# A two-block kernel: the first projection with the weights stationary, u made once, the fold done behind the projection

## The chip, the cores and the metric

One core of a Trainium2 chip runs the whole program in one launch. The metric is the device time of an execution in microseconds (us), the median of several runs. The engines are TensorE (PE; its weight loads are PEld), VectorE (DVE), ScalarE (ACT), GpSimd (POOL) and SyncE (SP), which issues most DMAs.

## What is computed

Two transformer-like blocks in a row. The change lies in the first projection, the Fourier branch and the k and v projection of the first block; cut to these, with b = 1:

```python
h = concatenate([meta_tokens, x])                  # 16 + 1024 positions, 1024 wide
u = rmsnorm(h, norm_g)
proj = u @ w_in                                    # f_in (512), f_gate, q, k (128), v (128), a_gate
fr = real(fftn(f_in, axes=(position, channel of a group of 64), norm="ortho"))
f_out = einsum("blgc,gcd->blgd", fr, w_fmix) + b_fmix, times silu(f_gate)
a_out = attention(rope(rmsnorm(q)), rope(rmsnorm(k)), v) * silu(a_gate)
h = h + concatenate([f_out, a_out]) @ w_out        # then a norm and the second block
```

The second block (stick-breaking attention, a gated convolution, a feed-forward part with w_up and w_down) takes most of the time and is not touched.

## The kernel before

Every product of full precision is made of three matmuls in fp32r: each operand is split into a high part, rounded to fp32r, and a low part, the rest, and `three` adds high x high, high x low and low x high (L667, L668, L669). Weights go through a staging pair and a ring of four slots: SyncE loads a chunk of 512 KB, GpSimd's `split` (L559 to L562) writes its high and low parts, and TensorE frees the slot with the semaphore w_used. SyncE loads chunk n once chunk n - 2 is split; GpSimd splits chunk c once chunk c - 4 has been used. Chunks 0 to 3 belong to the first projection, 4 to 7 hold the Fourier tables, 8 and 9 the k and v weights, then come the gates. The order on each engine is written out by hand, and waits are on counting semaphores.

The first 184 us go as follows. (1) x comes in as eight tiles of 128 tokens and one of 16 meta tokens. ScalarE squares and sums them (L1241) and guesses the reciprocal root (L1201, L1203), VectorE refines it in four small instructions (L1829 to L1832) and scales the tile (L1850), TensorE turns it (`transpose_tile`, L677), ScalarE copies it into `u_t` (L1233). (2) The real Fourier transform over 1040 positions needs only the sums and differences of position n and 1040 - n. VectorE forms them from `u_t` for each of the eight groups of 128 features (L1887, L1888), ScalarE and VectorE split them into `u_folded` (L1255, L1879). (3) `tm_units` projects: the folded u is the stationary operand, 512 columns of weights move. The 521 sums and 519 differences are ten row tiles; the fifth and the tenth hold only 9 and 7 rows. (4) Sixteen Fourier products of 15 matmuls, in two halves with eight channel products behind each; the fifth group of three is for the short rests, with `dft_tail`. VectorE makes low parts of the results (`dft`, L1927), then `f_out` (L1937, L1940). (5) x is loaded again, scaled again (L1850), and each tile is turned ahead of the kv unit before its own; the high and low parts of `u` are kept this time (L1311, L1855). (6) After the nine kv units the first two k tiles are turned (`turn_k`, L826), and the other seven amid the gate units, one after every fifteen matmuls; the third needs its rotation (`k_rotated`, L1971).

## Time and profile before

| | |
|---|---|
| median of 3 runs | 2212.61 us (2210.72 to 2220.72) |
| the profiled execution's own time | 2215.88 us |
| its span, first to last instruction | 2214.1 us |
| instructions | 27859 |
| mean granted TensorE clock | 0.985 |

A row of the timeline gives the start in us from the span's start, the busy time, the engine, the line, the instruction with the tiles it writes and reads, and in brackets the idle time of the engine just before with what ended it. Durations of overlapping matmuls are longer than the pitch from one start to the next; the pitch is what counts for a sum. The granted clock is 1.00 at 2.4 GHz and 0.50 at 1.2 GHz.

### The profile page before, as it was taken

The numbers are of one execution on the slowest core, as the hardware profiler recorded it, in microseconds if no ns is written. First come the engines' busy times: TensorE is split into PE (matmuls) and PEld (weight loads), VectorE is DVE, ScalarE is ACT, GpSimd is POOL, SyncE is SP. The second block draws the span as 40 slices with busy tenths as digits, with TensorE's granted clock in tenths as the row PEclk, the third lists the DMA queues.
The fourth block names the chain that finished last, engine by engine and source line by source line (L and its number), as shares of the span: only waits on it lengthen the run. The fifth ranks groups of instructions, "written<-read, shape, count | busy, mean of one in ns | idle before, by whom it ended". The sixth has DMA issues, their size and how long they took to land.

```text
span 2214.1 us, 27859 instructions
## 1 busy us (share of the span) xinstructions
PE 2115.9 (96%) x10545; PEld 1745.4 (79%) x10545; DVE 1113.4 (50%) x1608; ACT 840.4 (38%) x1485; POOL 749.0 (34%) x661
## 2 busy tenths in 40 slices
PE   5899999999999999999999999999999999999996
PEld 4587888999777788787877888878888888878785
DVE  7347657888353375766657652542222222221513
ACT  5124228999232364644545421432221222111212
POOL 3222142222233322322222244233333333367672
PEclk8999999999999999999999999999999999999998
DMA  5031120010142121111212543421111111132432
GB/s 173 21 123 50 58 95 30 11 46 11 60 143 71 55 66 48 57 56 53 71 48 80 173 143 105 133 86 48 47 47 47 47 47 47 47 106 94 153 103 76
DMA packets 142923, 164.69 MB, mean 74 GB/s; under 512 B 7091, under 2 KB 108999, under 8 KB 142823
## 3 DMA queue, kind: packets, MB, share of 16 engines
q1 hardware_dynamic: 118663, 98.10, 14.5%
q10 hardware_dynamic: 24160, 65.23, 8.4%
q8 instruction: 66, 1.08, 0.2%
q14 instruction: 34, 0.28, 0.0%
HBM read 133.94 MB, written 29.36 MB: 74 GB/s over the span
## 4 chain that ended last, share of the span: by engine, by line
PE 82%; DVE 9%; issue 5%; ACT 2%; DMA 1%; POOL 1%; ACTq 0%; DVEq 0%; POOLq 0%
PE psum L667 17%; PE psum L669 17%; PE psum L668 17%; PE psum L989 15%; PE psum L885 3%; PE psum L897 3%; PE psum L1026 1%; PE psum L916 1%; PE psum L917 1%; PE psum L918 1%; DVE softplus_part L2149 1%; PE psum L1010 1%; PE psum L1011 1%; PE psum L1043 1%; PE psum L677 1%
## 5 line engine op out<-in xcount | busy, mean ns | idle before, releaser
L559 POOL TENSOR_TENSOR w_ring<-w_staging,zero 128x8 fp32r<-128x8 f32 x172 | 47.6, 276 | 1204.2 <-PE psum L669 736.2
L562 POOL TENSOR_TENSOR w_ring<-w_staging,w_ring 128x1024 fp32r<-128x1024 f32 (+1 forms) x172 | 444.8, 2586 | 14.3
L989 PE MATMUL psum<-h,w_ring 128*128 128x512 f32 x1728 | 434.0, 401 | 0.7 <-ACT v L1503 0.7
L989 PEld LDWEIGHTS psum<-h,w_ring 128*128 128x128 f32 x1728 | 317.3, 190 | 67.9 <-ACT v L1503 1.1
L667 PE MATMUL psum<-ffn_in,w_ring 128*128 128x512 f32 x672 | 265.4, 395 | 0.0
L669 PE MATMUL psum<-ffn_in,w_ring 128*128 128x512 f32 x672 | 264.2, 393 | 0.0
L668 PE MATMUL psum<-ffn_in,w_ring 128*128 128x512 f32 x672 | 263.8, 393 | 0.0
L2282 DVE SCALAR_TENSOR_TENSOR up_buf<-psum,vectors,up_buf 128x1023 f32<-128x1023 f32 x44 | 56.4, 1283 | 309.7 <-ACT up_buf L1746 309.7
L560 POOL TENSOR_SCALAR w_ring<-w_staging 128x1016 fp32r<-128x1016 f32 (+1 forms) x172 | 183.5, 1067 | 0.0
L1746 ACT ACTIVATE up_buf<-psum,vectors 128x1024 f32<-128x1024 f32 x44 | 49.2, 1117 | 268.0 <-PE psum L669 267.9
L669 PEld LDWEIGHTS psum<-ffn_in,w_ring 128*128 128x128 f32 x672 | 126.0, 188 | 30.4
L668 PEld LDWEIGHTS psum<-ffn_in,w_ring 128*128 128x128 f32 x672 | 126.4, 188 | 29.3
L667 PEld LDWEIGHTS psum<-ffn_in,w_ring 128*128 128x128 f32 x672 | 126.0, 188 | 29.0
L667 PE MATMUL psum<-w_ring,ffn_split 128*128 128x512 f32 x352 | 140.5, 399 | 4.7 <-DVE ffn_split L2296 4.7
L669 PE MATMUL psum<-w_ring,ffn_split 128*128 128x512 f32 x352 | 140.0, 398 | 0.0
L668 PE MATMUL psum<-w_ring,ffn_split 128*128 128x512 f32 x352 | 139.7, 397 | 0.0
L2296 DVE TENSOR_TENSOR ffn_split<-ffn_mid,ffn_split 128x512 fp32r<-128x512 f32 x44 | 46.0, 1048 | 173.9 <-ACT ffn_split L1757 169.2
L2161 DVE TENSOR_TENSOR stick_w_t<-psum,stick_w_t 128x512 fp32r<-128x512 f32 (+3 forms) x96 | 53.3, 556 | 112.3 <-ACT stick_w_t L1580 112.2
L1757 ACT ACTIVATE ffn_split<-ffn_mid 128x512 fp32r (+1 forms) x44 | 27.7, 632 | 202.1 <-PE psum L669 185.5
L2149 DVE TENSOR_TENSOR_SCAN softplus_part<-one,softplus 128x128 f32<-128x128 f32 (+7 forms) x64 | 97.6, 1526 | 2.2
L1580 ACT ACTIVATE stick_w_t<-psum 128x512 fp32r<-128x512 f32 (+3 forms) x96 | 47.2, 492 | 129.7 <-PE psum L1026 128.5
L1458 ACT ACTIVATE probs<-psum,minus_max 128x348 f32<-128x348 f32 x192 | 91.7, 552 | 2.3 <-DVE minus_max L2075 1.9
(285 smaller groups left out, 4564.9 us busy)
## 6 DMA issues: line engine op xcount, KB each, us to landing
w_staging<-in_w_in SPq DMA_DIRECT2D x58, 512.0 KB, 3.8
w_staging<-in_w_up SPq DMA_DIRECT2D x44, 512.0 KB, 3.8
w_staging<-in_w_down SPq DMA_DIRECT2D x44, 512.0 KB, 3.2
w_staging<-in_w_out SPq DMA_DIRECT2D x16, 512.0 KB, 3.8
scratch_gates<-gate_out ACTq DMA_DIRECT2D x32, 256.0 KB, 2.6
merge_gates<-scratch_gates ACTq DMA_DIRECT2D x16, 512.0 KB, 4.5
x_again<-scratch_x ACTq DMA_DIRECT2D x16, 512.0 KB, 4.6
xin<-in_x ACTq DMA_DIRECT2D x8, 512.0 KB, 3.3
```

Of the source, the lines that this page charges most:

```text
L560: pool.tensor_scalar(hi[:, 0:w], WS[:, s, 0:w], 1.0, 0.0, ALU.mult, ALU.add).then_inc(S["w_hi"], 1)
L562: pool.tensor_tensor(lo[:, 0:width], WS[:, s, 0:width], plain(hi[:, 0:width]), ALU.subtract).then_inc(S["w_split"], 1)
L667: pe.matmul(dst, sh, mh, start=first, stop=False)
L668: pe.matmul(dst, sh, ml, start=False, stop=False)
L669: return pe.matmul(dst, sl, mh, start=False, stop=last)
L885: ins = pe.matmul(PB[:, b, 0:KPART], QS[:, h, P * t:P * t + P], k2[:, h // GROUP, KPART * b:KPART * (b + 1)], start=x == 0, stop=x == 1)
L897: ins = pe.transpose(PB[0:rows, 3 + g, P * (kt % 4):P * (kt % 4) + P], PR[:, i % 2, first:first + rows], IDENT[:, :])
L989: ins = pe.matmul(mix_bank(h), (sl if x == 2 else sh)[:, P * k:P * k + P], ml if x == 1 else mh, start=m == 0, stop=m == UNIT // 2 - 1)
L1458: act.activation(PR[:, i % 2, KPART * b:KPART * (b + 1)], PB[:, b, 0:KPART], ACT.Exp, bias=NB[:, i % 2:i % 2 + 1], scale=-1.0).then_inc(S[ ...
L2149: link(v.tensor_tensor_scan(ZL[:, i % 2, n - 1::-1], ONE[:, 0:1].broadcast_to([P, n]), ZS[:, i % 3, n - 1::-1], 0.0, ALU.mult, ALU.add))
L2161: v.tensor_tensor(WT[:, 1, 4 * g:4 * g + w, cols], PB[:, 4, 0:P * w].rearrange("p (k n) -> p k n", n=P), plain(WT[:, 0, 4 * g:4 * g + w, c ...
L2282: v.scalar_tensor_tensor(out=UB[:, g, 1:N_TOK], in0=up[:, 0:N_TOK - 1], scalar=w1, in1=UB[:, g, 1:N_TOK], op0=ALU.mult, op1=ALU.add).then_ ...
```

## The change

u is made once, in high and low parts, in the order meta tile, 0, 1, ... 7 (`FIRST`). The first projection now keeps the weights stationary and moves u: 16 units of 24 matmuls with 260 columns (`FIN`, unit (f, c) makes 128 features f at a quarter c of the positions). Only after the projection are the results folded (`fold`), turned by TensorE (`turn_folded`, ten transposes for each f) and split (`folded_hi`, `folded_lo`). The rests of sums and differences (9 rows each, high, high again and low) are stacked on the partitions 0, 32 and 64 of one tile, so that one matmul with 80 rows does what three did. The second loading, scaling and turning of x is gone, and with it the transposes amid the kv units; the order of k's work on ScalarE and VectorE is rewritten. x tiles and weight chunks are loaded in another order, and the rope table and gains through ScalarE's queue.

```diff
-N_U = 0
-N_A1 = N_U + KTILES
+FIRST = [(TT,)] + [(t, t + 1) for t in range(0, TT, 2)]
+FIRST_TILES = [t for group in FIRST for t in group]
+FIN = [(0, 0), (1, 0), (0, 1), (1, 1), (2, 0), (2, 1), (3, 0), (3, 1)] + [(f, c) for c in (2, 3) for f in range(4)]
+FIN_TILES = {1: (2, 3), 3: (4,), 4: (5,), 5: (6,), 6: (7,)}
...
-            for t in range(1, KTILES, 2):
-                sp.dma_start(XALL[0:tokens_of(t)[1], t, :], x_tile(t)).then_inc(S[f"x_in{t}"], 16)
+            sp.dma_start(IDENT[:, :], const["ident"]).then_inc(S["consts"], 16)
+            sp.dma_start(XALL[:, 1, :], x_tile(1)).then_inc(S["x_in1"], 16)
...
+                if c < 2:
+                    for t in ((3,), (5, 7))[c]:
+                        sp.dma_start(XALL[:, t, :], x_tile(t)).then_inc(S[f"x_in{t}"], 16)
...
-            for t in range(KTILES):
-                transpose_tile(N_U + t, N_U, N_U, tokens_of(t)[1])
+            def fin_unit(n):
+                f, c = FIN[n]
+                if c == 0:
+                    pe.wait_ge(S["w_split"], C_FIN + f + 1)
+                if f == 0:
+                    pe.wait_ge(S["nt_free"], 2 * c + 3)
+                if n >= 3:
+                    pe.wait_ge(S["fi_free"], n - 2)
+                sh, sl = slot(C_FIN + f)
+                for k in range(KT):
+                    mh, ml = (A1[:, x, k, HALF * c:HALF * (c + 1)] for x in range(2))
+                    ins = three(fin_bank(n), sh[:, P * k:P * k + P], sl[:, P * k:P * k + P], mh, ml, k == 0, k == KT - 1)
+                ins.then_inc(S["w_used" if c == 3 else "fi_mm"], 1)
+
+            def turn_folded(f):
+                if f:
+                    pe.wait_ge(S["fc_lo"], 3 * f)
+                for h in range(2):
+                    pe.wait_ge(S["fold_sum"], 3 * f + h + 2)
+                    for i in range(4):
+                        ins = pe.transpose(folded(h, i), FSUM[:, f % 2, h, P * i:P * i + P], IDENT[:, :])
+                    ins.then_inc(S["ft_mm"], 1)
+                for h in range(2):
+                    ins = pe.transpose(folded(2, h)[0:REST, :], FSUM[:, f % 2, h, 4 * P:FOLDS], IDENT[:, :])
+                ins.then_inc(S["ft_mm"], 1)
+
+            for t in (TT, 0, 1):
+                first_tile(t)
+            for n in range(8):
+                fin_unit(n)
+                for t in FIN_TILES.get(n + 1, ()):
+                    first_tile(t)
...
-            tm_units(T_FIN, 2 * NF, C_FIN, 4, FW, fold_stat, lead=4)
-            pe.wait_ge(S["tail_done"], 1)
-            pe.wait_ge(S["tm_free"], 2 * NF)
+            for n in range(8, 14):
+                fin_unit(n)
+            pe.wait_ge(S["rest_zero"], 3)
+            pe.wait_ge(S["cw_done"], 2)
+            turn_folded(0)
+            fin_unit(14)
+            turn_folded(1)
+            fin_unit(15)
+            turn_folded(2)
...
+                        if h == 0 and kind == 0:
+                            if ct == 2:
+                                turn_folded(3)
+                            pe.wait_ge(S["fc_lo"], 3 * ct + 3)
...
-                        for i in range(NF):
+                        for i in range(4):
...
+                        ins = pe.matmul(dst, FCT[0:REST_ROWS, kind, P * ct:P * ct + P], TAIL[0:REST_ROWS, 2 * h + kind, :],
+                                        start=False, stop=True)
...
-                pe.wait_ge(S["tm_free"], T_DFT + 16 * h + 8)
-                pe.wait_ge(S["cw_done"], 2)
...
-            settle(tm=T_KV)
-            for t in range(KTILES):
-                transpose_tile(N_A1 + t, N_A1, N_A1, tokens_of(t)[1])
-                if t:
-                    kv_unit(t - 1)
-            kv_unit(KTILES - 1)
+            for u in range(KTILES):
+                kv_unit(u)
...
+            def fold(f):
+                if f >= 2:
+                    v.wait_ge(S["ft_mm"], 3 * (f - 1))
+                v.wait_ge(S["fi_free"], 13 + f)
+                u, both = FRAW[:, f, :], FSUM[:, f % 2, :, :]
+                v.tensor_copy(both[:, 0, 0:FOLD + 1:FOLD], u[:, 0:FOLD + 1:FOLD]).then_inc(S["fold_sum"], 1)
+                v.tensor_tensor(both[:, 0, 1:FOLD], u[:, 1:FOLD], u[:, POS - 1:FOLD:-1], ALU.add).then_inc(S["fold_sum"], 1)
+                v.tensor_tensor(both[:, 1, 0:FOLD - 1], u[:, 1:FOLD], u[:, POS - 1:FOLD:-1],
+                                ALU.subtract).then_inc(S["fold_sum"], 1)
...
-    out = token_major(w1, 0, FW)
+    out = [feature_tile(w1, P * f) for f in range(4)]
```

First place: VectorE (DVE) at the program's start. Names ending in a number are buffers of the scaled tile (`xn`) and the gain. Before:

```order
L1829 TENSOR_SCALAR mean<-sumsq 128x2
L1830 SCALAR_TENSOR_TENSOR newton_a<-rsqrt_guess 128x2
L1831 TENSOR_TENSOR newton_b<-newton_a,mean 128x2
L1832 SCALAR_TENSOR_TENSOR rstd_x<-newton_b,rsqrt_guess 128x2
L1850 SCALAR_TENSOR_TENSOR xn_67<-x_tiles,rstd_x,gain_68 128x1024 x2
```

In the changed program, from the second refinement on (the meta tile is ahead of it):

```order
L1880 SCALAR_TENSOR_TENSOR rstd_x<-newton_b,rsqrt_guess 128x2
L1918 SCALAR_TENSOR_TENSOR xn_66<-x_tiles,rstd_x,gain_67 128x1024 x2
L1903 TENSOR_TENSOR u<-psum,u 128x8x16
L1877 TENSOR_SCALAR mean<-sumsq 128x2
L1878 SCALAR_TENSOR_TENSOR newton_a<-rsqrt_guess 128x2
L1879 TENSOR_TENSOR newton_b<-newton_a,mean 128x2
L1880 SCALAR_TENSOR_TENSOR rstd_x<-newton_b,rsqrt_guess 128x2
L1918 SCALAR_TENSOR_TENSOR xn_66<-x_tiles,rstd_x,gain_67 128x1024
L1903 TENSOR_TENSOR u<-psum,u 128x8x128 x2
L1918 SCALAR_TENSOR_TENSOR xn_66<-x_tiles,rstd_x,gain_67 128x1024
```

Before, this group came once for each pair of tiles with nothing between; now the low parts of u (L1903) stand among the scalings.

Second place: TensorE (PE) at the end of the first projection. The last unit before the Fourier products is followed in the changed program by the turning of a folded quarter (L770, L773):

```order
L671 MATMUL psum<-u,w_ring 128x260
L672 MATMUL psum<-u,w_ring 128x260
L673 MATMUL psum<-u,w_ring 128x260
L770 MATMUL psum<-ident,fold_sum 128x128 x8
L773 MATMUL psum<-ident,fold_sum 9x128 x2
L671 MATMUL psum<-u,w_ring 128x260
L672 MATMUL psum<-u,w_ring 128x260
```

Before, nothing but projection matmuls (L667 to L669) stood there; four such rounds of ten transposes are new, the last of them amid the Fourier products.

Third place: TensorE between the last channel product and the first kv unit. Before:

```order
L669 MATMUL psum<-dft,channel_w 128x260
L677 MATMUL psum<-ident,xn_67 128x128 x16
L667 MATMUL psum<-w_ring,u 128x256
L668 MATMUL psum<-w_ring,u 128x256
L669 MATMUL psum<-w_ring,u 128x256
```

In the changed program:

```order
L671 MATMUL psum<-dft,channel_w 128x260
L672 MATMUL psum<-dft,channel_w 128x260
L673 MATMUL psum<-dft,channel_w 128x260
L671 MATMUL psum<-w_ring,u 128x256
```

The sixteen transposes are gone from here, and the other tiles' from between the kv units.

## Rows read from the trace of the kernel before

**Rows 1.** The page's chain that ended last, share by engine.
```profile
PE 82%; DVE 9%; issue 5%; ACT 2%; DMA 1%; POOL 1%; ACTq 0%; DVEq 0%; POOLq 0%
```
**Rows 2.** Timeline of TensorE, 38 to 65 us.
```profile
38.44 3.45 PE L752 MATMUL psum<-w_fmix_blocks,channel_raw 128*128 128x512 f32 x4
41.25 0.87 PE L667 MATMUL psum<-w_ring,u_folded 128*128 128x512 f32 x1
...
63.93 0.39 PE L668 MATMUL psum<-w_ring,u_folded 128*128 128x512 f32 x1
64.17 0.40 PE L669 MATMUL psum<-w_ring,u_folded 128*128 128x512 f32 x1
```
**Rows 3.** Timeline of VectorE, 9 to 40 us.
```profile
9.53 2.48 DVE L1850 SCALAR_TENSOR_TENSOR xn<-x_tiles,rstd_x,gain 128x1024 f32<-128x1024 f32 x2
...
19.00 2.35 DVE L1831 TENSOR_TENSOR newton_b<-newton_a,mean 128x2 f32<-128x2 f32 x1
...
21.58 5.27 DVE L1850 SCALAR_TENSOR_TENSOR xn<-x_tiles,rstd_x,gain 128x1024 f32<-128x1024 f32 x2
...
38.98 0.70 DVE L1888 TENSOR_TENSOR fold_sum<-u_t 128x519 f32<-128x519 f32 x1
```
**Rows 4.** Timeline of GpSimd, 17 to 22 us.
```profile
17.66 0.20 POOL L559 TENSOR_TENSOR w_ring<-w_staging,zero 128x8 fp32r<-128x8 f32 x1 [16.76 <-DMA w_staging<-in_w_in]
...
18.95 2.38 POOL L562 TENSOR_TENSOR w_ring<-w_staging,w_ring 128x1024 fp32r<-128x1024 f32 x1
```
**Rows 5.** Timelines of GpSimd and VectorE at 117 us.
```profile
116.47 2.43 POOL L562 TENSOR_TENSOR w_ring<-w_staging,w_ring 128x1024 fp32r<-128x1024 f32 x1
...
117.28 0.43 DVE L1927 TENSOR_TENSOR dft<-psum,dft 128x260 fp32r<-128x260 f32 x1 [1.37 <-ACT dft L1277]
```
**Rows 6.** Timeline of TensorE, 70 to 108 us.
```profile
70.05 0.60 PE L667 MATMUL psum<-w_ring,u_folded 128*9 128x512 f32 x1 [5.49 <-DVE f_in L1916]
70.44 0.63 PE L668 MATMUL psum<-w_ring,u_folded 128*9 128x512 f32 x1
...
74.71 0.63 PE L669 MATMUL psum<-w_ring,u_folded 128*9 128x512 f32 x1
...
107.56 0.36 PE L667 MATMUL psum<-w_ring,f_in 128*128 128x260 f32 x1 [1.44 <-issue]
107.75 0.28 PE L668 MATMUL psum<-w_ring,f_in 128*128 128x260 f32 x1
107.87 0.28 PE L669 MATMUL psum<-w_ring,f_in 128*128 128x260 f32 x1
```
**Rows 7.** Timeline of TensorE, 123 to 184 us.
```profile
123.16 0.39 PE L667 MATMUL psum<-dft,channel_w 128*128 128x260 f32 x1 [0.94 <-DVE dft L1927]
...
145.43 0.28 PE L669 MATMUL psum<-dft,channel_w 128*128 128x260 f32 x1
147.64 2.29 PE L677 MATMUL psum<-ident,xn 128*128 128x128 f32 x16 [1.93 <-DVE f_out L1940]
151.11 0.38 PE L667 MATMUL psum<-w_ring,u 128*128 128x256 f32 x1 [1.18 <-DVE u L1855]
...
183.87 0.60 PE L826 MATMUL psum<-ident,k_rotated 128*64 128x128 f32 x4
```
**Rows 8.** Timeline of TensorE at 192 us.
```profile
192.04 0.63 PE L826 MATMUL psum<-ident,k_rotated 128*64 128x128 f32 x2 [4.10 <-DVE k_rotated L1971]
```
**Rows 9.** Timeline of VectorE, 149 to 190 us.
```profile
149.83 1.23 DVE L1855 TENSOR_TENSOR u<-psum,u 128x1024 fp32r<-128x1024 f32 x1 [1.05 <-ACT u L1311]
...
187.81 2.46 DVE L1994 TENSOR_TENSOR v_hi_ones_lo<-k_v,v_hi_ones_lo 128x128 fp32r<-128x128 f32 x1
```
**Rows 10.** Timeline of GpSimd at 188 us.
```profile
187.78 2.34 POOL L562 TENSOR_TENSOR w_ring<-w_staging,w_ring 128x1024 fp32r<-128x1024 f32 x1
```
**Rows 11.** Windows: busy us (instructions) of PE, PEld, DVE, ACT, POOL; granted clock; DMA share, GB/s.
```profile
18.00:34.00 16.00, 7.72 (x35) 6.52 (x34) 14.99 (x16) 9.01 (x19) 15.67 (x11) 0.50 0.58 161
107.00:147.00 40.00, 36.13 (x288) 34.94 (x288) 13.72 (x33) 10.04 (x24) 20.18 (x16) 1.00 0.34 107
```

More of the change, by code:

```diff
@@ L41 @@
 FOLD = POS // 2
-FOLDS = 522
-NF = 5
-REST = {0: FOLD + 1 - 4 * P, 1: FOLD - 1 - 4 * P}
+FOLDS = 521
+REST = FOLDS - 4 * P
+REST_HI = 32
+REST_LO = 64
+REST_ROWS = 80
 HALF = FOLD // 2
@@ L217, in tm_signals @@
 def tm_signals():
-    groups = [(2 * NF, C_FIN + 4)]
+    groups = []
     for h in range(2):
@@ L1226, in _, with first_guess @@
                     load_tables()
             nf = 2 * FT
-            def u_out(t):
-                first, rows = tokens_of(t)
-                act.wait_ge(S["nt_mm"], t + 1)
-                act.activation(UT[:, :, first:first + rows], pair_tiles(t % 2)[:, :, 0:rows],
-                               ACT.Copy).then_inc(S["nt_free"], 1)
-            for t in range(0, KTILES, 2):
-                both = range(t, min(t + 2, KTILES))
-                for x in both:
-                    rows = tokens_of(x)[1]
+            def first_guess(group):
+                rows = tokens_of(group[0])[1]
+                for x in group:
@@ L1248, in _ @@
+            first_guess(FIRST[0])
+            first_guess(FIRST[1])
+            first_hi(TT)
+            first_guess(FIRST[2])
+            first_hi(0)
+            first_hi(1)
+            first_guess(FIRST[3])
+            fin_out(0)
+            first_hi(2)
+            first_hi(3)
+            first_guess(FIRST[4])
+            for n in range(1, 8):
+                fin_out(n)
+                if 2 <= n < 6:
+                    first_hi(n + 2)
             act.wait_ge(S["nt_xn"], KTILES)
@@ L1343, in _ @@
+            for u in range(KTILES - 2, KTILES):
+                k_hi(u)
             for f in range(4):
@@ L1859, in _, with first_refine @@
             v.memset(WBD[:, :, :], 0.0).then_inc(S["cw_zero"], 1)
-            v.wait_ge(S["consts"], 16 * N_CONSTS)
-            for t in range(KTILES):
-                rows = tokens_of(t)[1]
-                if t % 2 == 0:
-                    n = min(2, KTILES - t)
-                    refine(rows, t, n, 1.0 / D, RX)
-                normalise(N_U, t, XALL[0:rows, t, :], RX[0:rows, t:t + 1], rows)
+            v.wait_ge(S["consts"], 32)
+            def first_refine(group):
+                refine(tokens_of(group[0])[1], group[0], len(group), 1.0 / D, RX)
@@ new lines, in _ @@
+            first_refine(FIRST[0])
+            first_norm(TT)
+            for g in range(1, len(FIRST)):
+                t, last = FIRST[g]
+                first_refine(FIRST[g])
+                first_norm(t)
+                if g > 1:
+                    first_lo(t - 2)
+                if g == 2:
+                    first_lo(t - 1)
+                first_norm(last)
+                if g == 1:
+                    first_lo(TT)
+                elif g > 2:
+                    first_lo(t - 1)
@@ L1911, in _ @@
                                      ROPER[:, 1, :, :].rearrange("p t (f e) -> p t f e", e=2), swapped, ALU.mult))
-            v.wait_ge(S["fpad"], 1)
-            for u in range(2 * NF):
-                h, _, rows = folded(u)
-                v.wait_ge(S["tm_hi"], u + 1)
-                v.tensor_tensor(FC[0:rows, 1, h, u % NF, :], PB[0:rows, tm_bank(T_FIN + u), :],
-                                plain(FC[0:rows, 0, h, u % NF, :]), ALU.subtract).then_inc(S["tm_free"], 1)
-            def again(t, rows):
-                n = N_A1 + t
-                v.wait_ge(S[f"nt_in{n % 2}"], 16 * (t // 2 + 1))
-                normalise(N_A1, t, XIN[N_A1][0:rows, n % 2, :], RX[0:rows, t:t + 1], rows)
+            v.wait_ge(S["v_chain"], chain[0])
+            for x in range(2):
+                v.memset(FSUM[:, x, 1, FOLD - 1:FOLDS], 0.0).then_inc(S["rest_zero"], 1)
+            fold(0)
+            fold(1)
+            folded_lo(0)
+            fold(2)
+            folded_lo(1)
+            fold(3)
+            folded_lo(2)
             for h in range(2):
@@ new lines, in _ @@
+            for u in range(KTILES):
+                rows = tokens_of(u)[1]
+                rotate(u, KSQ, rows, KV_HEADS)
+                v.wait_ge(S["kv_vhi"], u + 1)
+                v_lo = VV[0:rows, u, :, 2 * DH:3 * DH] if u < TT else VV[META_VLO:META_VLO + META, TT, :, 0:DH]
+                mark(v.tensor_tensor(v_lo,
+                                     KV[0:rows, u, P:2 * P].rearrange("p (g d) -> p g d", g=KV_HEADS),
+                                     plain(VV[0:rows, u, :, 0:DH]), ALU.subtract))
+                k_rotate(u)
+                if u >= 2:
+                    k_lo(u - 2)
@@ L2006, in _ @@
+            for u in range(KTILES - 2, KTILES):
+                k_lo(u)
             v.wait_ge(S["kv_kll"], 2 * KTILES)
```

309 lines of the change are left out of this document (141 added, 168 removed).

## The prediction

> **What bounds the kernel now.** I read the chain of work that ended last first: 82% of it is matmuls, spread over all stages [rows 1], so TensorE sets the time nearly everywhere, and what the change can win is TensorE work and TensorE waits in the stretch it touches, 0 to 184 us; behind it nothing of the instruction streams changes, so the rest should only move earlier. In that stretch TensorE's timeline [rows 2, 6, 7, 8] gives five segments. (A) The first projection does not start before 41.25 us; before that there are tile transposes with gaps [rows 2]. What it waits for is VectorE's chain: normalise nine tiles from 9.53 us on, then fold [rows 3]. (B) From 41.25 to 107.56 it runs 240 matmuls of 512 columns, at a pitch of 0.232 us (63.93 to 64.17), with one wait of 5.49 us for VectorE, after which the pitch is 0.427 us (70.44 to 74.71, ten steps), the lower of the two clock levels [rows 2, 6]. 48 of the 240 matmuls produce only 9 or 7 rows of result. (C) Fourier products and channel products from 107.56 to 145.43 at a pitch of 0.12 us for 260 columns [rows 6, 7]. (D) A hole with two tile transposes until the kv projection starts at 151.11 [rows 7]. (E) kv until 183.87, with a tile of u turned before each unit (two of them together last 2.29 us at 147.64) [rows 7]. Then (F) a wait of 4.10 us for the third k tile, at 192.04 [rows 8].
>
> **The change, segment by segment.** Durations are those of the profiled execution (span 2214.1, own time 2215.88 us); the median of the runs is 3.3 us lower, and I carry differences over to it.
>
> *A, start.* The fold leaves the path: the projection now needs only the meta tile and tiles 0 and 1, split into high and low parts, and one weight chunk. By counting VectorE's queue up to tile 1's low part: three refinements of about 0.65 us, the meta tile's scaling and three of tiles (2.48 for two [rows 3]), low parts at 1.23 each [rows 9] and 0.3 for the meta tile; together 9.7 us. The gain vector and the first guess allow a start at about 8.8 (today the first scaling stands at 9.53, one refinement later [rows 3]). Without disturbance that is 18.5 us. But the weights now stand third in SyncE's queue, ahead of five tiles of x, so GpSimd no longer starts its splits at 17.66 [rows 4]; I estimate 9 us for chunk 0 and 15 us for chunk 1. One split takes 3.6 us (17.66 to the end of the 2.38 us that start at 18.95 [rows 4]), and while it runs VectorE is held up: the 128x2 product at 19.00 took 2.35 us and ended with the GpSimd row of 18.95, and the two tiles at 21.58, beside the next split, took 5.27 instead of 2.48 us [rows 3, 4]. The subtraction from PSUM is not held up: 0.43 us at 117.28, inside GpSimd's 116.47 to 118.90 [rows 5]. Two splits fall wholly into VectorE's 9.7 us: 18.5 + 7.2 = 25.7 if all is serial; some of it meets low parts and waits, so I take 23, with 18.5 and 27 (part of a third split) as ends. The Trainium skill says the same in "SBUF — State Buffer", Who interferes with whom: a VectorE instruction with two SBUF inputs and a GpSimd instruction that reads SBUF exclude each other for the whole instruction, and one with a single SBUF input goes free. The trace agrees, and by that rule alone, with no overlap, the start would be the 25.7. Change of A: 23 - 41.25 = **-18.3**.
>
> *B, first projection.* 16 units of 24 matmuls with 260 columns: 384 x 0.120 = 46.1 us. Six tile transposes between them: in segment E seven of them, one small, and their short waits fill 32.8 - 25.7 = 7.1 us (below), so about 0.93 us a tile, 5.6. The small transposes and the channel product, which used to be ahead of 41.25 [rows 2], come inside: 2.2 (3.45 us at the lower clock, faster at the higher). Three of the four rounds that turn the folded f_in, ten transposes each at 0.93 / 8 us: 3 x 1.16 = 3.5. Lower clock for the first unit: a pitch of 0.427 x 260 / 512 = 0.217 instead of 0.120, 24 x 0.097 = 2.3, as after the two waits in rows 6 and 8. Waits: unit 2 needs tile 3's low part, which VectorE can only reach after the transposes of tiles 2 and 3 that stand behind unit 0 (two scalings and two low parts, 5 us, against 1 us of transposes and 2.9 of unit 1): 1.2; turned banks 0.5. Sum 61.4 against 66.3 us: **-4.9**. All fold work (2 x 0.70 us a quarter [rows 3] and a small copy) lies under the units that follow; the copies of each unit out of PSUM too, with three banks against 2.9 us a unit. The moved DMAs of the rope table and gains go out on ScalarE's queue while unit 8 runs; their users have 15 us. If that cover fails the fold of quarter 0 is late, and TensorE waits ahead of unit 14.
>
> *C, Fourier and channel products.* Each unit loses 2 of 15 matmuls: 16 x 2 x 0.12 = -3.8. Ahead of the channel products the wait for all eight evacuations (0.94 us idle ahead of 123.16 [rows 7]) is narrowed to the banks: -0.8 twice. Added: the fourth turning round, 1.15, and in its neighbourhood the chain unit 15, copy, fold, turn, high part, low part (about 0.6 + 1.6 + 1.2 + 2.2 + 1.8 = 7.4 us) that must end before column tile 3 may start: TensorE has only some 5.5 us of other work in it, so about 2.0 of wait. Sum: **-2.2**.
>
> *D.* The second making of u is gone; kv starts one bank release after the last channel product: 5.5 becomes 0.3, **-5.2** [rows 7].
>
> *E.* No transposes amid kv: 9 x 24 x 0.119 = 25.7 against 32.8: **-7.1** [rows 7].
>
> *F.* k's tile 2 must still pass ScalarE and VectorE after the last kv copy. Two tiles' worth of v work is already done, but GpSimd splits two gate chunks at the same place, and VectorE's subtraction at 187.81 took 2.46 us with GpSimd's row of 187.78 beside it [rows 9, 10]. Serial with those splits I get k turned about 8.1 us after kv's end, today 8.2: **0**. Ends: 0 and -6.4 (the wait and the slower matmuls behind it both gone: the work itself without GpSimd is 3.4 us, and TensorE arrives after 3.9).
>
> Sum: -18.3 - 4.9 - 2.2 - 5.2 - 7.1 = **-37.7**. Own time 2215.9 - 37.7 = 2178.2; at the median 2212.6 - 37.7 = **2174.9**, say 2175.
>
> **Rivals.** *1, the start is held longer and the clock stays low.* VectorE and GpSimd exclude each other throughout, the first unit starts at 27 (+4), and the short waits between units 0 to 3 keep TensorE at the lower level for three more units (3 x 2.3 = +6.9). For it: transposes with gaps between 18 and 34 us stand at the lower level today, granted clock 0.50 [rows 11]. Against: under full work it is at the higher one, a pitch of 0.23 for 512 columns at 64 us [rows 2]. It gives about 2186. *2, the k wait goes away.* If the splits are met in another order, F brings -4 to -6.4, and with a start at 20 the time is 2175 - 5 - 3 = 2167. Against it: the same two splits hang on the same kv unit. *3, nothing comes of it.* VectorE's and ScalarE's chain through the projection could become the bound: per tile 1.24 + 1.23 us on VectorE, per quarter 1.6 + 1.8; all together about 24 us for nine tiles, 14 for four quarters and 7 for tables, 45 us of work in 60, so it would have to stand idle for the whole gain of 37.7: about 2212. *4, slower.* One mechanism: 260 columns a matmul are too few for TensorE to be kept at the higher level. Then 384 + 208 matmuls cost 0.097 us more each, +57.4, of which 2.3 is counted already: 2175 + 55 = 2230. It decides when over 37.7 / 0.097 = 390 of these matmuls run at the lower level. Against it: today's 260-column products stand at a pitch of 0.12 with a granted clock of 1.00 [rows 6, 11].
>
> **How the numbers follow.** The forecast (-33 to -43 us) gets 0.61; its own range is 2169 to 2180. Rival 1: 0.19. Rival 2: 0.14. Rival 3: 0.03. Rival 4: 0.03. The range must reach over rivals 1 and 2: lower end 2163, upper end 2188, which leaves about 0.1 in the no-gain cases and tails beyond each of those rivals. A measurement of this kernel tells about 0.5%, 11 us, from no change; so faster 0.94, same 0.03, slower 0.03.
>
> **What would show it.** In the changed profile: the first 260-column matmul at about 23 us (18.5 to 27); GpSimd's first split at about 9 us and VectorE rows of 2 us and more beside it; first Fourier product at about 84; a wait of some 2 us around column tiles 2 and 3 of the first Fourier group; no hole ahead of kv, kv ending at about 146, and still a wait of about 4 us for the third k tile, the rest of the program in its old durations, some 38 us earlier. The prediction is wrong if the first unit starts after 30, if the units take more than 3.2 us each on the mean, or if a stage behind the gates changes its length.

## The result, and the profile after

The changed kernel takes 2181.22 us, the median of 4 runs (2180.59 to 2182.41), against 2213.98 us of the kernel before in the same comparison (4 runs, 2210.72 to 2220.72). The ratio is 0.9849 with a 95% interval of 0.9825 to 0.9873, or 32.8 us less; 2175 was forecast, in 2163 to 2188. The profiled execution took 2181.48 us with a span of 2179.3, so the two profiles stand 34.8 us of span apart (34.4 of own time). The execution profiled before was 1.9 us above its median and this one 0.3 above, which makes the 1.6 us between 34.4 and 32.8.

The page of the changed kernel: span and instructions, busy time of each engine, and the chain's share by engine, to be held against [rows 1].

```profile
span 2179.3 us, 27963 instructions
PE 2094.6 (96%) x10625; PEld 1744.4 (80%) x10625; DVE 1085.6 (50%) x1575; ACT 828.6 (38%) x1482; POOL 746.9 (34%) x661
PE 85%; DVE 8%; ACT 3%; issue 2%; DMA 1%; POOL 1%; ACTq 0%; SPq 0%; DVEq 0%; POOLq 0%
```

Matmuls have gone from 82% to 85% of the chain, and "issue" from 5% to 2%. TensorE's busy time fell from 2115.9 us to 2094.6, by 21.3, and the span by 34.8, so that work left the path as well as 13.5 us of idle time. The segments can be read off the timeline of TensorE in the changed kernel. Its rows answer to [rows 2, 6, 7, 8].

```profile
24.94 0.56 PE L671 MATMUL psum<-u,w_ring 128*128 128x260 f32 x1 [8.22 <-DVE u L1903]
...
36.57 0.39 PE L671 MATMUL psum<-u,w_ring 128*128 128x260 f32 x1 [1.15 <-DVE u L1903]
...
79.09 0.66 PE L770 MATMUL psum<-ident,fold_sum 128*128 128x128 f32 x4 [1.59 <-DVE fold_sum L1931]
...
88.41 0.37 PE L671 MATMUL psum<-w_ring,f_in 128*128 128x260 f32 x1
...
121.68 0.28 PE L673 MATMUL psum<-dft,channel_w 128*128 128x260 f32 x1
121.98 0.39 PE L671 MATMUL psum<-w_ring,u 128*128 128x256 f32 x1
...
147.55 0.60 PE L868 MATMUL psum<-ident,k_rotated 128*64 128x128 f32 x4
...
155.69 0.60 PE L868 MATMUL psum<-ident,k_rotated 128*64 128x128 f32 x2 [4.06 <-DVE k_lo_lo L2051]
155.94 0.77 PE L671 MATMUL psum<-u,w_ring 128*128 128x512 f32 x1
...
161.67 0.38 PE L868 MATMUL psum<-ident,k_rotated 128*64 128x128 f32 x2
```

The reader takes differences of starts: the first unit to the first Fourier product, that to the last channel product, the hole, kv to the first k turn.

| segment | before | after | change | forecast |
|---|---|---|---|---|
| A: start of the first unit | 41.25 | 24.94 | -16.3 | -18.3 |
| B: first projection | 66.3 | 63.5 | -2.8 | -4.9 |
| C: Fourier and channel products | 37.9 | 33.3 | -4.6 | -2.2 |
| D: hole ahead of kv | 5.7 | 0.3 | -5.4 | -5.2 |
| E: kv | 32.8 | 25.6 | -7.2 | -7.1 |
| sum at the first k turn | 183.87 | 147.55 | -36.3 | -37.7 |
| F: third k tile, from kv's end | 8.17 | 8.14 | 0.0 | 0 |

At the last turning of k the two programs are 215.94 - 180.49 = 35.45 us apart. The 0.9 between this and 36.3 lies behind the third k tile: its fifteen matmuls last 161.67 - 155.94 = 5.7 us here, 4.8 before (192.32 to 197.13), for more of them run at the lower clock. Windows of the changed kernel: busy us (instructions) of PE, PEld, DVE, ACT, POOL, then granted clock, DMA share and GB/s.

```profile
26.00:30.00 4.00, 4.00 (x20) 4.00 (x20) 3.58 (x4) 0.00 (x0) 3.92 (x4) 0.50 0.19 42
...
40.00:60.00 20.00, 20.00 (x160) 18.85 (x159) 8.52 (x8) 6.30 (x11) 0.00 (x0) 1.00 0.07 15
```

Unit 0 runs at 0.50 (1.2 GHz); from then on the 260-column matmuls have the full 2.4 GHz, as the window from 40 to 60 shows, 160 of them in 20 us. What held the start and one fold stands in VectorE's timeline of the changed kernel:

```profile
16.96 0.92 DVE L1877 TENSOR_SCALAR mean<-sumsq 128x2 f32<-128x2 f32 x1 [2.58 <-ACT rsqrt_guess L1241]
...
19.26 3.27 DVE L1918 SCALAR_TENSOR_TENSOR xn<-x_tiles,rstd_x,gain 128x1024 f32<-128x1024 f32 x1
22.45 2.34 DVE L1903 TENSOR_TENSOR u<-psum,u 128x1024 fp32r<-128x1024 f32 x2
...
76.10 2.93 DVE L1931 TENSOR_TENSOR fold_sum<-f_in_t 128x519 f32<-128x519 f32 x1
...
85.56 1.28 DVE L1938 TENSOR_TENSOR f_in<-psum,f_in 128x512 fp32r<-128x512 f32 x2
...
148.56 1.71 DVE L2059 TENSOR_TENSOR v_hi_ones_lo<-k_v,v_hi_ones_lo 128x128 fp32r<-128x128 f32 x1
...
151.57 2.33 DVE L2028 TENSOR_TENSOR k_normed<-k_v,rstd 128x128 f32<-128x128 f32 x1
```

and GpSimd's, beside it:

```profile
14.18 0.20 POOL L563 TENSOR_TENSOR w_ring<-w_staging,zero 128x8 fp32r<-128x8 f32 x1 [13.29 <-DMA w_staging<-in_w_in]
...
19.10 2.34 POOL L566 TENSOR_TENSOR w_ring<-w_staging,w_ring 128x1024 fp32r<-128x1024 f32 x1
...
75.65 2.83 POOL L566 TENSOR_TENSOR w_ring<-w_staging,w_ring 128x1040 fp32r<-128x1040 f32 x1
...
85.17 2.77 POOL L566 TENSOR_TENSOR w_ring<-w_staging,w_ring 128x1040 fp32r<-128x1040 f32 x1
...
151.42 2.34 POOL L566 TENSOR_TENSOR w_ring<-w_staging,w_ring 128x1024 fp32r<-128x1024 f32 x1
```

The low parts of tiles 0 and 1 (22.45), which the first unit waits for, stand on VectorE behind the refinement of tiles 2 and 3, and that stood still until 16.96, for ScalarE's guess. ScalarE could square tile 3 only when it had landed, as its own timeline shows:

```profile
15.31 1.06 ACT L1267 ACTIVATE junk<-x_tiles 128x1024 f32<-128x1024 f32 x1 [1.67 <-DMA x_tiles<-in_x]
```

### The profile page after: what moved, and what is told of

The parts are those of the page before. It is cut to its first block, busy times and chain, and to the rows that moved or that the text cites. A ratio compares the mean times of both kernels' runs of the same rounds, so it can differ in the third digit from the quotient of the medians.

```text
span 2179.3 us, 27963 instructions
## 1 busy us (share of the span) xinstructions
PE 2094.6 (96%) x10625; PEld 1744.4 (80%) x10625; DVE 1085.6 (50%) x1575; ACT 828.6 (38%) x1482; POOL 746.9 (34%) x661
## 4 chain that ended last, share of the span: by engine, by line
PE 85%; DVE 8%; ACT 3%; issue 2%; DMA 1%; POOL 1%; ACTq 0%; SPq 0%; DVEq 0%; POOLq 0%
PE psum L671 18%; PE psum L673 18%; PE psum L672 18%; PE psum L1027 15%; PE psum L923 3%; PE psum L935 3%; PE psum L1064 1%; PE psum L954 1%; PE psum L955 1%; PE psum L956 1%; DVE softplus_part L2210 1%; PE psum L1048 1%; PE psum L1049 1%; PE psum L681 1%; PE psum L1081 1%
## 5 line engine op out<-in xcount | busy, mean ns | idle before, releaser
L671 PE MATMUL psum<-u,w_ring 128*128 128x260 f32 (+1 forms) x256 | 91.1, 356 | 9.5 <-DVE u L1903 9.4
```

The costliest lines, as they stand in the source:

```text
L671: pe.matmul(dst, sh, mh, start=first, stop=False)
```

## The experiments

Each kernel is the changed one with the edit shown. Comparisons were made in several groups, each with its own runs of the kernel before. Runs of one kernel spread by 2 to 7 us (those of the kernel before by up to 10), so a difference of 1 or 2 us between medians is not read as a gain or a loss; where it matters, the traces are compared, place by place. Each kernel has one trace, and these differ too: in six traces without an edit ahead of the Fourier products these start between 87.1 and 88.5 us. Three questions were open: why the first unit came 2 us late, whether GpSimd's splits are what stretches VectorE's rows and keeps the k wait, and whether the terms of C and E are what they seem. The rival to each is that the wait belongs to something else.

### The start: low parts ahead of the refinement (e1_start_order)

```diff
             first_hi(TT)
-            first_guess(FIRST[2])
             first_hi(0)
             first_hi(1)
+            first_guess(FIRST[2])
...
                 t, last = FIRST[g]
+                if g == 2:
+                    first_lo(t - 2)
+                    first_lo(t - 1)
                 first_refine(FIRST[g])
                 first_norm(t)
-                if g > 1:
+                if g > 2:
                     first_lo(t - 2)
-                if g == 2:
-                    first_lo(t - 1)
```

> The changed kernel, with the high and low parts of tiles 0 and 1 made ahead of the sums, guess, refinement and scaling of tiles 2 and 3, on ScalarE and on VectorE. Theory (order): the first projection unit starts at 24.94 us because VectorE's queue holds the low parts of tiles 0 and 1 behind a refinement that waits until 16.96 us for tile 3 to land, and then behind a scaling held up by GpSimd. With the order turned the start is one high and one low part behind tile 1's transposes (16.7 + 1.1 + 1.3): 19.0 to 20.0 us, and most of the 5 us reach the end: 2181.2 becomes 2176 to 2178. Rival (weights and GpSimd hold the start whatever the order): start above 23 us and a time within 1 us of the changed kernel. Second rival (given back): start at 19 to 20, but tiles 2 and 3 come later, units 1 and 2 wait for them, and the time stays above 2179.

Measured: 2178.09 us (4 runs, 2175.53 to 2180.73) against 2213.54, ratio 0.9837 (0.9816 to 0.9857). Timeline of TensorE in this kernel:

```profile
18.94 0.36 PE L671 MATMUL psum<-u,w_ring 128*128 128x260 f32 x1 [2.46 <-DVE u L1903]
...
32.34 0.39 PE L671 MATMUL psum<-u,w_ring 128*128 128x260 f32 x1 [4.11 <-DVE u L1903]
...
85.72 0.37 PE L671 MATMUL psum<-w_ring,f_in 128*128 128x260 f32 x1
```

The first unit starts 6.0 us earlier, near the 18.5 that the prediction had as the lower end. So what held it was the order of the queues: the low parts stood behind tile 3's landing and behind a scaling that a split stretched. The edit moves them ahead of both, so it doesn't tell the two apart. But the first Fourier product comes only 2.7 us earlier. Unit 2 waits 4.11 us instead of 1.15 for tile 3's low part, and starts 4.2 us earlier, not 6.0 (32.34 against 36.57). Another 1.5 us go behind this wait: from the ninth matmul on, some 14 of unit 2's matmuls stand at a pitch of 0.217 (granted clock 0.50), where the changed kernel has 0.12. The median is within the 2176 to 2178 expected; its interval overlaps that of the changed kernel.

### The start: tile 3 loaded first (e5_start_queue)

```diff
             sp.dma_start(XALL[:, 1, :], x_tile(1)).then_inc(S["x_in1"], 16)
+            sp.dma_start(XALL[:, 3, :], x_tile(3)).then_inc(S["x_in3"], 16)
...
-                    for t in ((3,), (5, 7))[c]:
+                    for t in ((), (5, 7))[c]:
```

> The changed kernel, with x's tile 3 loaded ahead of the first weight chunk; the order on the engines is the changed kernel's. Theory (tile 3's landing holds VectorE's second refinement, 16.96 us): it lands about 1.5 to 2.5 us earlier, the split of the chunk comes as much later, and the first unit starts at 22 to 24 us instead of 24.94; time 2179 to 2181. Rival (GpSimd's splits decide): they now stand later in the scalings and low parts, start 24.5 or later, no gain.

Measured: 2181.82 us (2179.11 to 2182.7) against 2213.0, ratio 0.9857 (0.984 to 0.9873): as the changed kernel. Timeline of TensorE:

```profile
23.30 0.56 PE L672 MATMUL psum<-u,w_ring 128*128 128x260 f32 x1 [6.42 <-DVE u L1904]
...
36.13 0.59 PE L672 MATMUL psum<-u,w_ring 128*128 128x260 f32 x1 [2.74 <-DVE u L1904]
```

1.6 us are won at the first unit and lost at unit 2 (a wait of 2.74, and slower matmuls behind it); the Fourier products start at 90.18, later than the 88.41 of the changed kernel. So the landing was a part of what held the start: VectorE's second refinement begins at 15.49 instead of 16.96, though beside GpSimd's row of 16.28 one of its products of 128x2 elements takes 2.37 us. An earlier landing alone gives nothing in the end.

### The start: fill the wait as well (e10_units_first)

e1 with another order of units: all four feature groups on the quarters 0 and 1, then on the others. So four units, not two, are to be had from each landed pair of tiles.

```diff
-FIN = [(0, 0), (1, 0), (0, 1), (1, 1), (2, 0), (2, 1), (3, 0), (3, 1)] + [(f, c) for c in (2, 3) for f in range(4)]
+FIN = [(f, c) for c in range(4) for f in range(4)]
```

> The start order of the first experiment, and the first projection's units in the order of position quarters: all four feature tiles of quarter 0 first. Theory: in the first experiment 4.11 us of the 6 gained at the start were lost at unit 2, which waits for tile 3's low part; with two more units that need only tiles 0 and 1 in front of it this wait is filled. First unit at 19 us, wait ahead of the first unit of quarter 1 under 1.5 us, Fourier products start at 82 to 83 instead of 85.7 (88.4 in the changed kernel), time 2174 to 2176. Rival: the units of feature tiles 2 and 3 wait for their weight chunks, which GpSimd finishes at 28 and 33 us, and the start of the Fourier products stays above 85.

Measured: 2177.01 us (2173.02 to 2179.71) against 2215.94, ratio 0.9826 (0.9811 to 0.9842). Timeline of TensorE:

```profile
19.93 0.36 PE L671 MATMUL psum<-u,w_ring 128*128 128x260 f32 x1 [2.46 <-DVE u L1903]
...
80.62 0.37 PE L671 MATMUL psum<-w_ring,f_in 128*128 128x260 f32 x1
```

Between the first unit and the Fourier products no wait above 1 us is left but the one at the fold of quarter 0 (1.60 us at 71.80), and the Fourier products start 7.8 us before those of the changed kernel. So what the wait at unit 2 took back in e1 is to be had with other work in its place. The span of this profile is 2172.6 us, 6.7 less than 2179.3; the median is 4.2 us less, and single runs spread by nearly 7; 2174 to 2176 had been expected.

### k: splits held back (e2_k_gate)

GpSimd waits with its next splits of gate chunks until the third k tile is rotated. They start at 151.14 instead of 146.40.

```diff
+            pool.wait_ge(S["pr_rope"], 3)
             run(peeled, C_OUT + 3, 1)
```

> The changed kernel, with GpSimd's split of the third gate chunk held back until k's third tile is rotated (the chunk is needed some 25 us later). Theory (VectorE and GpSimd exclude each other): VectorE's subtraction of 1.71 us and its scaling of 2.33 us around 149 to 154 us fall back to 0.28 and 0.29, the third k tile is turned 4 to 4.8 us after kv's end instead of 8.14, TensorE waits under 1 us instead of 4.06 and stays at the higher clock, which together is worth 3.3 + 2 = 4 to 6 us: 2175 to 2177. Rival (the chain itself takes the 8 us, whatever GpSimd does): turned at 7 us or later behind kv's end, time within 1 us of 2181.

Measured: 2181.57 us (2180.18 to 2183.22), ratio 0.9849 (0.9831 to 0.9867): no change, where 2175 to 2177 had been expected. Timeline of TensorE, then of VectorE and of GpSimd in this kernel:

```profile
151.65 0.38 PE L869 MATMUL psum<-ident,k_rotated 128*64 128x128 f32 x2 [0.21 <-DVE k_lo_lo L2052]
...
160.14 0.61 PE L869 MATMUL psum<-ident,k_rotated 128*64 128x128 f32 x2 [4.61 <-DVE k_lo_lo L2052]
```

```profile
148.34 0.29 DVE L2060 TENSOR_TENSOR v_hi_ones_lo<-k_v,v_hi_ones_lo 128x128 fp32r<-128x128 f32 x1
...
152.47 2.40 DVE L1879 SCALAR_TENSOR_TENSOR newton_a<-rsqrt_guess 128x2 f32<-128x2 f32 x1
...
156.38 2.31 DVE L2036 TENSOR_TENSOR k_times_cos<-k_normed,rope 128x128 f32<-128x128 f32 x1
```

```profile
152.43 2.43 POOL L566 TENSOR_TENSOR w_ring<-w_staging,w_ring 128x1024 fp32r<-128x1024 f32 x1
...
156.10 2.44 POOL L566 TENSOR_TENSOR w_ring<-w_staging,w_ring 128x1024 fp32r<-128x1024 f32 x1
```

The cause of the third tile's wait is shown: without a split beside them the v subtraction takes 0.29 us instead of 1.71, and the third tile's wait falls from 4.06 to 0.21 us. As soon as the splits run, a step on 128x2 elements takes 2.40 us and ends with GpSimd's row (154.87 against 154.86), and a product of 128x128 takes 2.31. (The Trainium skill has this in "SBUF — State Buffer", Who interferes with whom: a VectorE instruction with two SBUF inputs contends with a GpSimd instruction that reads SBUF. The trace agrees. The prediction took from there that an instruction with a single SBUF input goes free, and that is too wide: the section excepts the 2-port modes, which copies and `tensor_scalar` can enter. No run here shows the mode, but `mean`, a TENSOR_SCALAR with one input, took 2.38 us at 25.91 in the changed kernel, beside GpSimd's row of 24.82.) The wait has only moved to the fourth tile, and has even grown to 4.61: VectorE needs 3.4 us a tile (from 148.13 to 151.53, undisturbed), the distance between two turns on TensorE is 3.7 (162.79 - 159.08 in e9), so there are only some 0.3 us a tile in which it could catch up.

### k: the turns one step later (e9_k_later)

Each of the seven k turns amid the gate units stands 30 matmuls later; GpSimd's splits stay where they are.

```diff
-                if i % 5 == 4 and i // 5 + 2 < KTILES:
-                    turn_k(i // 5 + 2)
+                if i % 5 == 4 and 2 <= i // 5 < KTILES:
+                    turn_k(i // 5)
```

> The changed kernel, with the seven k turns amid the gate units each ten k steps (30 matmuls, 7 us) later; GpSimd's splits stay where they are. Theory: the second experiment only moved the wait from the third to the fourth k tile, since VectorE takes 3.4 us a tile and TensorE 3.7 between turns, so 3.7 us of a split always come out as a wait; with 7 us of slack TensorE never waits for k. Waits of 4.06 us gone, the clock stays at the higher level: the gates end 4 + 1 to 2 us earlier, 2175 to 2177. Rival (the wait moves again, to the gate copies or the q turns, since ScalarE's gate work stands behind k's): 2179 or more, with a new wait of 2 us and more before 250 us.

Measured: 2180.19 us (5 runs, 2176.07 to 2181.33) against 2215.94, ratio 0.9833 (0.9818 to 0.9849). Timeline of TensorE:

```profile
159.08 0.38 PE L868 MATMUL psum<-ident,k_rotated 128*64 128x128 f32 x2
...
178.39 0.38 PE L868 MATMUL psum<-ident,k_rotated 128*64 128x128 f32 x2 [0.52 <-DVE k_lo_lo L2051]
...
186.53 0.50 PE L671 MATMUL psum<-u,w_ring 128*128 128x512 f32 x1 [1.79 <-DVE gate_e L2073]
...
188.07 0.63 PE L673 MATMUL psum<-u,w_ring 128*128 128x512 f32 x1
```

The third tile is turned without a wait, and no stretch at the lower clock follows it. Counted from the first k turn, matmul by matmul, the kernel is 5.7 us ahead of the changed one when all k tiles are turned, the wait of 0.52 already paid. Then 3.6 of it go: 2.0 at the wait of 1.79 us for VectorE's gate work, and 1.6 behind it, where eight matmuls stand at a pitch of 0.43 (from 187.65 to 190.98) instead of 0.23. The edit has moved work on TensorE only, so VectorE has as much to do for k and the gates as before. By its time, 2179 or more, the expectation's rival came out, and not the 2175 to 2177 of the theory; its new wait was 1.79 us, a little under the 2 that it named. At ScalarE's table load behind the gates the trace is 1.7 us ahead (286.22 against 287.95); the medians say 1.0, within their spread.

### Fold: splits held back (e3_fold_gate)

GpSimd waits with the first Fourier chunk's split until the first quarter is folded.

```diff
+                if c == C_DFT:
+                    pool.wait_ge(S["fold_sum"], 3)
                 split(c, c % 2, *slot(c), w_dram[c][0], staged[c % 2], c - 3 if c >= 4 else None)
```

> The changed kernel, with GpSimd's split of the first Fourier chunk held back until the first quarter is folded. Theory (exclusion): VectorE's subtraction of 2.93 us at 76.10 falls to 0.7 and TensorE's wait of 1.59 us at 79.09 goes. But the split then meets the fold of the second quarter, so that half or more of it is given back before the Fourier products start at 88.41: start of those 87 to 88.3, time 2180 to 2181. Rival (no give-back): Fourier products start at 86.8, time 2179.6. Rival (no exclusion): the 2.93 us stay.

Measured: 2183.58 us (2179.94 to 2186.47), ratio 0.9859 (0.9837 to 0.9881). Timelines of VectorE and TensorE:

```profile
75.11 0.69 DVE L1933 TENSOR_TENSOR fold_sum<-f_in_t 128x519 f32<-128x519 f32 x1
...
77.29 2.38 DVE L1931 COPY fold_sum<-f_in_t 128x2 f32<-128x2 f32 x1 [1.48 <-ACT f_in_t L1285]
```

```profile
83.53 1.09 PE L772 MATMUL psum<-ident,fold_sum 128*128 128x128 f32 x8 [2.73 <-DVE f_in_rest L1944]
...
90.09 0.37 PE L673 MATMUL psum<-w_ring,f_in 128*128 128x260 f32 x1
```

The subtraction of quarter 0 takes 0.69 us instead of 2.93, and the first turning has no wait. But the splits start 1.55 us later (75.89 instead of 74.34), and meet quarter 1: its copy of 128x2 elements takes 2.38 us. The second turning waits 2.73 us, much of unit 15 behind it runs at a pitch of 0.217 (the lower clock), and the Fourier products start 1.7 us later than in the changed kernel. Quarter 3 is hit as well: its subtraction takes 2.92 us (at 91.14, beside GpSimd's row of 90.69), and TensorE waits 2.31 us at 95.76. The expectation had the collision with quarter 1, but only as giving back half or more of 1.6 us, with a start at 87 to 88.3; more than all was given back, for it left out the lower clock and quarter 3.

### kv with transposes again (e4_turns_kept)

Behind each of the first eight kv units eight transposes are made, whose results nothing reads.

```diff
                 kv_unit(u)
+                if u < TT:
+                    for k in range(KT):
+                        pe.transpose(pair_tiles(1)[:, k, :], IDENT[:, :], IDENT[:, :])
```

> The changed kernel, with eight transposes of the identity into two idle banks behind each of the first eight kv units, as many as stood there before the change; nothing reads them. Theory: TensorE alone bounds the kv stage, so each group costs 0.93 us: the stage grows from 25.6 to 33.0 us, the time by 7 to 7.5 us, to 2188.5. That would show the whole of the segment's gain to be TensorE's own instructions. Rival (part of the gain was the second scaling and splitting of u on the other engines): growth of 5 us or less, or much more than 8 us if the engines behind it get into step with it.

Measured: 2186.46 us (2182.24 to 2189.2), ratio 0.9869 (0.9846 to 0.9891). Timeline of TensorE:

```profile
122.11 0.39 PE L671 MATMUL psum<-w_ring,u 128*128 128x256 f32 x1
...
125.06 1.03 PE L888 MATMUL psum<-ident 128*128 128x128 f32 x8
...
154.79 0.60 PE L868 MATMUL psum<-ident,k_rotated 128*64 128x128 f32 x4
```

The stage lasts 154.79 - 122.11 = 32.7 us, against 25.6 in the changed kernel and 32.8 in the one before. Eight rounds of eight transposes cost 7.1 us, 0.89 each. That the stage comes out as long as before is in part chance, for before the change only six rounds of eight full transposes and one of eight small ones (16x16, at 177.15) stood inside it. Two rows of the kernel before:

```profile
172.95 1.09 PE L677 MATMUL psum<-ident,xn 128*128 128x128 f32 x8
...
181.05 0.29 PE L667 MATMUL psum<-w_ring,u 128*16 128x256 f32 x1 [0.20 <-DVE u L1855]
```

Six full rounds at 0.89 are 5.3 us, and the small one takes some 0.7. The other 1.1 or so of the 7.2 us are gaps in the last three units: the sixth round starts only at 172.95, when VectorE's scaling of 171.62 has ended (1.28 us), and the last unit waits for its low part of u. So about 6 us of the gain E are TensorE's own instructions, and about 1 us was waiting for the second making of u. The median is 5.2 us up, with a spread of 7 us in this kernel's runs; 2188.5 had been expected.

### The rests unstacked in time (e6_rest_extra)

Two extra matmuls of 80 rows ahead of each Fourier unit's group; their result is written over.

```diff
+                        for _ in range(2):
+                            pe.matmul(dst, FCT[0:REST_ROWS, kind, P * ct:P * ct + P], TAIL[0:REST_ROWS, 2 * h + kind, :],
+                                      start=True, stop=True)
                         for i in range(4):
```

> The changed kernel, with the stacked rest matmul issued three times instead of once in each of the sixteen Fourier units (the two extra ones come first and are overwritten by the group that follows). Theory: TensorE bounds the Fourier products, so 32 matmuls of 260 columns bring back 32 x 0.12 = 3.8 us: 2185.0. Rival (the evacuation behind each unit sets the pace, 0.39 and 0.43 us a unit): less than 1.5 us.

Measured: 2183.01 us (2181.95 to 2188.07), ratio 0.9866 (0.9848 to 0.9884). Timeline of TensorE:

```profile
87.88 0.48 PE L823 MATMUL psum<-dft_tail,f_in_rest 80*128 80x260 f32 x2
...
125.52 0.39 PE L671 MATMUL psum<-w_ring,u 128*128 128x256 f32 x1
```

37.6 us from the first Fourier product to kv instead of 33.6, so 4.1 us for 32 matmuls; the term said 32 x 0.12 = 3.8. In the median it is 1.8 us, less than the runs spread; 2185.0 had been expected.

### Both gates, and the changed kernel again (e7_start_and_k, e8_control)

e7 joins the edits of e1 and e2; e8 is the changed kernel without an edit.

> The changed kernel with both the start order of the first experiment and the held-back split of the second. If both theories hold and the gains add, 9 to 11 us: 2170 to 2173. If the start's gain is given back by the tiles behind it, 2175 to 2177. If both rivals hold, 2181.

> The changed kernel itself once more, on the same chip as the three others of this call: 2181 us within 1.5, so that the differences of the others can be taken against it.

Measured: e7 2181.48 us (2180.08 to 2184.18), ratio 0.9856 (0.984 to 0.9872); e8 2181.28 us (2179.29 to 2184.39), ratio 0.9855 (0.9839 to 0.9872). e8 gives the changed kernel's time within 0.1 us. In e7 the first unit starts at 18.76, but unit 2 stands for 6.07 us until 34.52, 2 us more than in e1, though the instructions there are the same; the fourth k tile waits 4.60 us, as in e2. VectorE's rows tell where the 2 us lie: of the short steps and scalings ahead of tile 3's low part, one at 25.40 takes 2.42 us where e1 has 0.89, one at 24.31 takes 1.00 instead of 0.17, and the scaling at 31.09 takes 2.23 instead of 1.27, each beside a split; the scaling at 28.05 is 1.4 us shorter than e1's. So small shifts of GpSimd against VectorE change this wait; what shifted them can't be said from one trace of each. By the time, the case came out in which nothing is gained (2181), though neither theory's mechanism failed: both gains were made at their place and given back behind it.

### The three edits that help, together (e11_all_three)

The edits of e10 (with e1's) and of e9.

> Start order, unit order and later k turns together. If the gains of the two before add: 6 and 5.5 us, 2169 to 2171. If one is given back: 2175.

Measured: 2173.68 us (2170.15 to 2174.55) against 2215.94, ratio 0.9808 (0.9794 to 0.9821). This is the fastest of all, 7.5 us below the changed kernel's 2181.2, and its slowest run is below every run of the changed kernel. Its ratio's interval, too, lies clear of the changed kernel's 0.9825 to 0.9873; it is the only one of these kernels of which that can be said. The time lies between the two that were expected, 2169 to 2171 and 2175. Timeline of TensorE:

```profile
19.08 0.36 PE L671 MATMUL psum<-u,w_ring 128*128 128x260 f32 x1 [2.47 <-DVE u L1903]
...
33.78 0.39 PE L671 MATMUL psum<-u,w_ring 128*128 128x260 f32 x1 [1.46 <-POOL w_ring L566]
...
179.82 0.50 PE L671 MATMUL psum<-u,w_ring 128*128 128x512 f32 x1 [1.80 <-DVE gate_e L2074]
```

TensorE's waits of over 1 us between 18 and 185 us are four in each kernel, the fold's of 1.6 us (79.09 in the changed kernel, 72.48 here) in both. With it they sum to 8.22 + 1.15 + 1.59 + 4.06 = 15.0 us there and 2.47 + 1.46 + 1.60 + 1.80 = 7.3 here. Of the 7.7 us won, the profile's span shows 6.9 (2172.4 against 2179.3). The wait at 33.78 is for a split weight chunk, which is what the rival in e10's expectation named.

## Why the prediction was right, and where its terms were off

**The main claim holds.** The stretch up to the k turns brought 36.3 of the forecast 37.7 us, the segments have the signs that were given and all but C (-4.6 for -2.2) and B (-2.8 for -4.9) nearly the size, and the rest of the program moved earlier almost as a block (34.8 at the end of the span).

**A was 2.0 us too large, right in the mechanism that it named and lacking a second one.** The 23 was made of 18.5 us of VectorE's work and 4.5 for two splits, with chunk 0 at 9 us. The chunk was there at 14.18, so the first splits fell later, and they added 3.6 us to VectorE's rows (0.8 each to those of 16.96 and 18.07, 2.0 to the scaling at 19.26). Besides, VectorE stood 2.58 us for tile 3's statistics, a wait that the sum had at nothing, for I had counted three refinements without asking when tile 3 lands (ScalarE got it at 15.31). That the miss is only 2.0 us is in part luck: a split term that was 0.9 too large hid a part of the missing wait. Two things that the text held apart, "the loads" and "VectorE's queue", met in one instruction: the refinement of tiles 2 and 3 stands ahead of the low parts that the first unit needs. e1 took the refinement and the stretched scaling from there, and the start fell to 18.94. The stretching by a split was of the kind foreseen: the scaling at 19.26 took 3.27 us beside GpSimd's 19.10 to 21.44.

**B was 2.1 us too large.** The wait before unit 2 was 1.15 us (1.2 forecast). The wait at quarter 0's fold was not in the sum: I had put all fold work under the units behind it, and named its failure as a wait "ahead of unit 14". That is where it came, 1.59 us at 79.09, for the subtraction at 76.10 took 2.93 us beside GpSimd's row of 75.65, where [rows 3] have 0.70. I had the exclusion in A and F and left it out here. The remaining 0.5 us I haven't assigned.

**C was 2.4 us too small.** The wait of 2.0 near column tiles 2 and 3 wasn't there (0.23 us). The chain from unit 15 on is hidden, so the sum without this wait, -4.2, is what the trace shows (-4.6). e6 puts the stacked rests at 4.1 us against 3.8.

**D and E were right to 0.2 us.** The sum took the hole D as 5.5 us, and it was 5.7 (145.43 to 151.11). For E, e4 gives the price of a round of transposes, 0.89 us, so that about 6 of the 7.2 us are transposes and 1 short waits. The prediction had both in its 7.1 together, and by dividing it put a round at 0.93.

**F was right: no gain, a wait of 4.06 us.** The releaser is another one. Before it was the rotation, now it is the low part of the first k tile (L2051), which stands on VectorE behind the third tile's rotation; that was ready at 154.76, and TensorE went on at 155.69. e2 shows that the splits make this wait, and also that rival 2 would not have paid if it had come about like this: the wait moves on by one tile. Behind it the lower clock lasted 0.9 us longer in effect than before; I had taken it as equal.

**Rival 1** (start at 27, three more slow units) lies outside what came: only unit 0 ran at 0.50. **Rival 4** is refuted by the window from 40 to 60 us, 1.00 with 260 columns. **Rival 3** is refuted by the result; the chain through the projection held TensorE for 1.15 and 1.6 us once it had started.

**The time** came out 6.3 us above the sum's 2174.9: 1.4 are the sum's own error, 0.9 lie behind the third k tile, 0.6 more up to the end of the span, 0.4 around it, 1.6 are the two profiled executions' distances from their medians, over which I had carried the difference unchanged, and 1.4 the median before, 2214.0 in this comparison and 2212.6 in the runs that I subtracted from. The first two are errors about the kernel; the 0.6 I haven't placed, and each of the others is smaller than the spread of one kernel's runs.

## What to carry to other kernels

When work leaves the path at the start of a program, the next limit is an order: list for the first instruction of the bottleneck engine what stands ahead of its last input in every queue, and when each of these inputs lands; here over half of what an edit of the start alone had won was lost at and behind the second wait, and kept once other work filled it (6.0 us earlier gave 2.7 at the Fourier products, with another order of units 7.8). Holding GpSimd's splits back moved the collision with VectorE and didn't remove it, in e2 as in e3. What helped was slack at the consumer, by turning later or by giving it other work, and that only in part: e9 alone kept 1.7 us in its trace, and only the edits of the start, the unit order and the turns together stand clear of the runs' spread. Every estimate of a short VectorE instruction in such a place should be made twice, with and without a whole GpSimd instruction in front of it.

## What the runs showed of the hardware that was not expected

How small an instruction may be and still be held: a copy of 128x2 elements took 2.38 us in e3 (0.17 without GpSimd beside it), a scalar-tensor-tensor of 128x2 2.40 us in e2 (0.15). The low parts with one operand in PSUM go free: the two of 128x512 at 85.56 took 1.28 us in the midst of GpSimd's row of 85.17 to 87.94, and the same two at 89.11, beside none of GpSimd's long rows, 1.27.

What one wait costs beyond itself: in the changed kernel the matmuls of 512 columns behind the wait of 4.06 us stand at a pitch of 0.427 from 156.52 to 160.36 (granted clock 0.50 from 156.5 to 160.4), then at 0.233 again. The length of the wait alone doesn't tell whether this comes. It came behind waits of 2.74 us (36.13 in e5) and 2.73 us (83.53 in e3), and a few matmuls behind those of 1.79 and 1.80 us in e9 and e11; it did not come behind 1.59 us (79.09, where the pitch stays 0.12), nor behind 2.31 us (95.76 in e3).
